# An attention stage on one core: TensorE multiplies the identity by a table before it waits for the prompt's scaled scores, and once at the stage's beginning

## The reference, cut to what matters

```
logits = einsum('bqgrd,bjgd->bgrqj', qn, kn) + bias      # selected and window branch
p = masked_softmax(logits, mask)
o = gates[0] * o_c + gates[1] * o_s + gates[2] * o_w      # o_x = p @ v of each branch
```

## Time and profile before

| | |
|---|---|
| time, median of 3 runs | 1291.38 us (1289.93, 1291.38, 1296.14) |
| span of the profiled execution | 1291.9 us |
| its own time | not among the three; the span lies 0.5 us above their median |
| TensorE busy | 1210.7 us, 94% of the span |
| VectorE busy | 467.1 us, 36% |
| ScalarE busy | 282.3 us, 22% |
| mean granted TensorE clock | 0.982 of full speed |
| attention with this change's places | from about 594 to 788 us of the span |

### The profile page before, as it was taken

The page is one execution under the profiler, slowest core; times in us unless marked ns, Lnnn a source line. Parts: engine busy times, 40 slices in busy tenths (PEclk is TensorE's granted clock), DMA queues, the critical chain, the costliest instruction groups (busy, mean ns, idle before and its releaser), DMA issues.

```text
span 1291.9 us, 38852 instructions
## 1 busy us (share of the span) xinstructions
PE 1210.7 (94%) x16250; PEld 1006.9 (78%) x16250; DVE 467.1 (36%) x1372; ACT 282.3 (22%) x757; POOL 197.9 (15%) x335
## 2 busy tenths in 40 slices
PE   7999999999999998997787879989999999999998
PEld 5887786999999976574345457787898888978876
DVE  2110115677774331004676763421221211212213
ACT  1000003101010021235876861210010000100122
POOL 3012122012340000233345440000000000000000
PEclk9999999999999998999898989999999999999999
DMA  9786879998344264464477776498988879889831
GB/s 311 292 324 238 303 264 314 181 371 311 113 150 175 104 260 177 143 126 137 145 254 217 228 251 252 175 409 330 388 308 346 334 302 394 312 317 367 321 128 37
DMA packets 108352, 326.44 MB, mean 253 GB/s; under 512 B 15512, under 2 KB 33769, under 8 KB 106516
## 3 DMA queue, kind: packets, MB, share of 16 engines
q1 hardware_dynamic: 90868, 263.71, 55.2%
q0 software_dynamic: 16160, 59.96, 15.4%
q10 hardware_dynamic: 1152, 0.30, 0.1%
HBM read 316.65 MB, written 14.52 MB: 256 GB/s over the span
## 4 chain that ended last, share of the span: by engine, by line
PE 87%; DVE 5%; issue 3%; ACT 2%; DMA 1%; POOLq 0%; POOL 0%; ACTq 0%; DVEq 0%
PE bank L1944 20%; PE bank L2543 15%; PE bank L2046 12%; PE pbank L2554 6%; PE bank L2082 6%; PE bank L2000 5%; PE pbank L2543 3%; PE bank L2554 3%; PE bank L2525 3%; PE bank L2150 2%; PE bank L2512 1%; PE bank L2177 1%; PE bank L2317 1%; PE bank L2272 1%; PE pbank L2512 1%
## 5 line engine op out<-in xcount | busy, mean ns | idle before, releaser
L2543 PE MATMUL bank<-X,gring 128*64 128x96 f32 x4608 | 196.0, 247 | 6.1 <-issue 6.1
L2543 PEld LDWEIGHTS bank<-X,gring 128*64 128x64 f32 x4608 | 191.9, 137 | 10.6 <-issue 10.6
L1944 PE MATMUL bank<-aT,gring 128*128 128x288 f32 x768 | 192.7, 410 | 3.5 <-DVE aT L1286 3.5
L1944 PEld LDWEIGHTS bank<-aT,gring 128*128 128x128 f32 x768 | 146.6, 192 | 46.0 <-issue 5.8
L2554 PE MATMUL pbank<-Q,X 128*32 128x256 f32 x1152 | 76.0, 379 | 0.0
L2046 PE MATMUL bank<-aT,gring 128*128 128x144 f32 x528 | 72.1, 286 | 0.0
L1865 DVE TENSOR_TENSOR hT<-hT,bank 128x288 f32<-128x288 f32 x48 | 18.9, 448 | 146.4 <-PE bank L2512 146.4
L2000 PE MATMUL bank<-Q,X 128*64 128x64 f32 x2048 | 63.3, 223 | 7.9 <-issue 7.9
L2000 PEld LDWEIGHTS bank<-Q,X 128*64 128x64 f32 x2048 | 61.3, 138 | 11.9 <-issue 11.5
L1872 DVE TENSOR_TENSOR X<-X,bank 128x96 f32<-128x96 f32 x72 | 18.4, 256 | 141.5 <-ACT X L1232 140.9
L2046 PEld LDWEIGHTS bank<-aT,gring 128*128 128x128 f32 x528 | 67.7, 190 | 0.0
(11 more groups left out here) (380 smaller groups left out, 1814.7 us busy)
## 6 DMA issues: line engine op xcount, KB each, us to landing
gring<-in_moe SPq DMA_DIRECT2D x176, 512.0 KB, 5.7
Q<-in_moe SPq DMA_DIRECT2D x72, 512.0 KB, 7.0
gring<-in_dense_gu SPq DMA_DIRECT2D x44, 512.0 KB, 13.4
Q<-in_cache_cmp POOLq DMA_DIRECT2D x64, 256.0 KB, 5.7
Q<-in_cache_cmp SPq DMA_DIRECT2D x64, 256.0 KB, 5.6
gring<-in_conv_in SPq DMA_DIRECT2D x24, 512.0 KB, 10.2
gring<-in_dense_down SPq DMA_DIRECT2D x16, 704.0 KB, 5.4
gring<-in_ple_gate SPq DMA_DIRECT2D x16, 512.0 KB, 5.6
```

What stands on the lines that cost most here:

```text
L1944: ins = pe.matmul(bank(label, k)[:, 0:T], tile[:, 128 * i:128 * i + 128], rhs[:, i, :], start=i == 0, stop=i == C - 1)
L2543: ins = pe.matmul(m_bank(i, M_GU + f)[64 * w:64 * w + 64, CAP * u:CAP * u + CAP], gslot(("m", 0), 2 * f + u)[:, o:o + 64], ae[:, c, :], st ...
```

## The change: what it does

A helper `kept_busy(dst, n)` issues n multiplications of the 128 x 128 identity by the first 512 columns of `tabP_` into a whole bank. Nothing reads their result; the work that follows starts its own sums in the bank. Eight stand ahead of the three waits at the stage's beginning, behind a wait for the bank of `("sc", 0)` and for `bias_in`. Four stand in each `prompt_transposes(k, 0)`, eight times in all, between `pair_free` and the wait for `pscaled`, into `pbanks[0]`. That is 8 + 8 x 4 = 40 multiplications. Nothing is removed and no other engine's list changes.

```
+            def kept_busy(dst, n):
+                for _ in range(n):
+                    pe.matmul(dst[:, 0:512], ident[:, :], tabP_[:, 0:512], start=True, stop=True)
+
+            bank_free(pe, ("sc", 0))
+            pe.wait_ge(bias_in, 16)
+            kept_busy(bank(("sc", 0)), 8)
             pe.wait_ge(kn_ready, 8)
             pe.wait_ge(q_ready, 8)
             pe.wait_ge(kcn_ready, 3)
...
                 pair_free(pe, k, T0 + i)
+                if i == 0:
+                    kept_busy(pbanks[0], 4)
                 pe.wait_ge(pscaled, 5 * k + (3 if i == 0 else 5))
```

## The result

The changed kernel takes 1313.36 us (median of 4 runs, 1312.55 to 1315.78) against 1292.84 us before in the same comparison: a ratio of 1.0162 with a 95% interval of [1.0137, 1.0188], 17.7 to 24.3 us slower. The prediction said 1300.9 us, 1295.5 to 1305.5. The direction was right; the forecast change, +9.5 us, is less than half of the measured 20.9.

The account below looks back on a forecast made before the run. TensorE, holding 87% of the chain, was taken as the bound. The terms +0.2 - 3.8 + 0.3 + 3.4 + 2.6 + 3.4 + 3.4 sum to +9.5 us: a median of 1300.9 us, range 1295.5 to 1305.5.

Parts of the forecast that it names:

- Price at full clock: TensorE: one added multiplication is two rows of 0.427 us, 0.85 us; four cost 3.41 us.
- Rival D: All places: multiplications are four times as cheap; -0.4 us in all, 1291.0 us; chance 0.05.
- Pair 7: T0 of pair 7: TensorE has no wait there, so the four cost +3.4 us.
- Pairs 1, 3 and 5: T0 there: the four start behind the drain, with nothing left to wait for; +3.4, +2.6 and +3.4 us.
- The cover at pair 3: After pair 3: ScalarE's 1.32 us wait for a DMA hides 0.8 us of the cost, leaving +2.6.
- Pair 6: T0 of pair 6: -0.5 us at full clock, +1.3 if the clock has fallen; taken as +0.3.
- Pair 0: T0 of pair 0: the four prevent the clock's fall over 7.60 us of half-speed work; -3.8 us.
- Rival A: Pair 0: the clock falls all the same; +13.3 us in all, 1304.7 us; chance 0.16.
- Pairs 2 and 4: T0 there: the late start and the half-speed stretch are both covered by VectorE's queue; 0 us.
- Beginning: Stage's beginning: the eight end 1.9 us past the present start, but the clock doesn't fall; +0.2 us.
- Rival B: Half-speed stretches of pairs 1, 3 and 5 go too, saving 4.9 us; +4.6 in all, 1296.0 us; chance 0.15.
- Rival C: Multiplications lie inside the waits everywhere in the loop, odd pairs cost 0.4 each; net -8.6 us, 1282.8 us; chance 0.05.

Follow-up runs that it names:

- e8: Kernel before plus eight multiplications, instead of four, in T0 of pairs 1, 3 and 5 only: 1.0189, +24.4 us.
- e10: Kernel before plus only the four multiplications of pair 7: 1.0031, +4.0 us.
- e3: Kernel before plus only the four multiplications in T0 of pairs 1, 3 and 5: 1.0106, +13.7 us.
- e9: Kernel before plus, at pairs 1, 3 and 5, three multiplications ahead of pair_free and four behind it: 1.0074, +9.6 us.
- e4: Kernel before plus only the four multiplications in T0 of pairs 6 and 7: 1.0045, +5.8 us.
- e16: Kernel before plus only the four multiplications of pair 6: 1.0018, +2.3 us.
- e11: Kernel before plus only the four multiplications of pair 0, first timing: 0.9969, -4.0 us.
- e15: Kernel before plus only the four multiplications of pair 0, second timing: 0.9984, -2.1 us.
- e2: Kernel before plus only the four multiplications in T0 of pairs 0, 2 and 4, first timing: 1.0004.
- e14: Kernel before plus only the four multiplications in T0 of pairs 0, 2 and 4, second timing: 0.9997.
- e13: Kernel before plus only the four multiplications of pairs 2 and 4: 0.9990.
- e1: Kernel before plus only the eight multiplications at the stage's beginning: 1.0004, +0.5 us.
- e5: The kernel before, unchanged, timed once more like a change: 1.0000, runs from 1284.09 to 1296.98 us.
- e6: Kernel before plus three multiplications ahead of pair_free at pairs 1, 3 and 5, into the samples' transposes' bank: 1.0011.

## Why the prediction was wrong, step by step

**Price at full clock: right.** 0.85 us forecast; e8 gives 0.89 from times, pair 7 0.86 from its trace (3.43 us for four). The forecast's row, (7.03 - 0.17) / 16, is 0.429 us and not 0.427, which changes nothing. Rival D falls with it.

**Pair 7: right.** +3.4 forecast; +3.4 in the trace, +4.0 [1.3, 6.7] in e10.

**Pairs 1, 3 and 5: the place was right, the size wrong, and this is the step that failed.** The prediction said "The half-speed stretch lasts until 661.0 in both; only what runs in it changes, so the price is 3.41 at full clock, not more." The stretch did last as long as before. But the step assumed that the transposes, once relieved of the low clock, would give back all that the multiplications lose in it. In the changed kernel the four took 5.2 us at each of the three pairs, 1.8 more than at full clock. From T0 to the next keys it is 3.87 us before (658.20 to 662.07) and 3.38 after (664.21 to 667.59), 0.5 given back; at pairs 3 and 5 it is 4.16 and 4.21 before and 3.38 after, 0.8 given back. What limits it is VectorE: T1 starts 0.1 us behind the last of the four copies in both kernels (661.08 and 666.60), so slow transposes that ran beside the copies had cost little. The prediction named that limit at pair 6 and left it out here. The last copy and T1 of pair 1 in the trace of before:

```profile
660.55 0.42 DVE L1619 COPY X<-pbank 128x256 f32<-128x256 f32 x1
661.08 1.06 PE L2257 MATMUL pbank<-ident,aT 128*128 128x128 f32 x8
```

So the account is 5.2 - 0.5 = +4.7 at pair 1 and 5.2 - 0.8 = +4.4 at pairs 3 and 5, together +13.5; where nearly all four fall into the stretch, as at pair 1 of e3, it is 6.5 - 0.5 = +6.0. e3 measured +13.7 for three where the prediction's terms sum to 9.4; e9, with the four at the high clock, gives +9.6, the price that I had forecast. The two times alone differ by no more than their intervals allow; with the traces of the three places beside them the step is shown.

**The cover at pair 3: nearly absent.** I took 0.8 us from ScalarE's wait for a DMA; at that place +4.5 was lost, with 0.6 back by pair 4.

**Pair 6: too low; the bad case was the usual one.** +0.3 forecast, a value between full clock (-0.5) and a bad case of +1.3 in which the clock has fallen. In e4 and e16 the bad case came as described, with 5.2 us for the four and +1.2 in the trace. In the changed kernel it was worse: the clock fell in TensorE's pause, near 776.1 us, before the four began at 776.92, and stayed low for all of them: 6.5 us, and +2.7 by the table. By time, e16 has +2.3.

**Pair 0: mechanism right, but a gain of one trace, not of the kernel; this is the second step that failed.** -3.8 forecast, -3.4 in the trace. But without the four the long stretch is there in 7 of 11 profiles, so the average gain is 2.3 us by the traces; e11 and e15 measured -4.0 and -2.1, while e2 and e14, with pairs 2 and 4 added, measured +0.5 and -0.4. How much of the gain a time shows stays open. I had reasoned from the one execution as if it were all of them. The Trainium skill (TensorE: Matmul & The Clock Gate, section What's actually happening) says that the slow phase varies from run to run with the same kernel. These profiles agree: the fall at pair 0 lasted some 10.2 us in 7 of 11 and was short or missing in the others. Rival A was no better: the clock didn't fall there in any of the six profiles with the four.

**Pairs 2 and 4: right.** VectorE covers them, e13.

**Beginning: not contradicted** (+0.2 forecast, +0.5 in e1, but with an interval from -2.1 to +3.0 that is no test of it). It is near +2.3 by the two traces with the clock low ahead of it, the changed kernel's and e5's: the wait without the eight is then 3.2 us and not 5.0.

**Rival B** falls twice: the half-speed stretches of pairs 1, 3 and 5 stayed in the changed kernel, and in e6, where they are gone, they are worth nothing measurable, against the 4.9 us which I gave them. **Rival C** falls with the rows at pairs 1, 3 and 5 of the changed kernel: the multiplications start when the drain ends, with no wait behind them.

The change is 20.9 us where 9.5 was forecast. By the four parts e1 to e4 the missing 11.4 are 4.3 in the odd pairs, 4.3 in pairs 0, 2 and 4 (+0.5 for a forecast of -3.8), 2.1 in pairs 6 and 7, 0.3 at the beginning, and 0.4 left over. With the single places put in (0.5 + 13.7 + 2.3 + 4.0 - 2.1, with e15 for pair 0 and pairs 2 and 4 at nothing) the sum is 18.4 us, and 16.5 with e11's -4.0; that is less than 20.9, but within the intervals of the terms. The trace of the changed kernel against that of before has 16.5 of its 19.0 us in the attention's parts: 4.2 more than forecast in the odd pairs, 2.4 more at pair 6, and only 0.4 of gain missing at pair 0, since that one trace of before had the long stretch.

## What to carry to other kernels

Work put in to fill a wait belongs ahead of the last semaphore to be released, not between two of them: find which of the waits ends last at each place, for a helper called eight times may have three of one kind and four of another. Filler that starts behind a pause may itself run at the low clock, here 5.2 to 6.5 us for four that cost 3.4 at full clock, and what it hands on at the high clock is worth only what the next engine in line lets through. A half-speed stretch in one profile is one throw of the dice: before a gain is booked on it, look whether it is there, and as long, in other executions of the same program.

## What the runs showed of the hardware that was not expected

- The kernel before varies by 1% from run to run (1283 to 1299 us over some hundred runs, one far outlier aside). The mean granted clock varies too, from 0.976 to 0.985 in the last 35 of them: the same small multiplications (L2210, L2217) run at 1.00 in one execution and at 0.50 in another (5.4 us of the changed kernel's trace).
- TensorE fully busy didn't always raise the clock. In the kernel before it stayed at 0.50 through 7.60 us of unbroken work on L2272 to L2317; behind the pauses of pairs 1 and 3 it was back within about 3.4 us of the fall.
- The same four multiplications took 3.4, 5.2 or 6.5 us. At pair 6 of the changed kernel nearly all of them lay at 0.50 (the window from 776.2 to 782.9, busy for 5.98 us); those at pair 1 began at 1.00, the clock was 0.50 from 660.1 to 663.4, and they ended at 1.00. How long filler stays slow isn't fixed by the filler.
- Without the four, the fall behind T0 of pair 0 lasted some 10.2 us in seven profiles, 3.4 in three, and was missing in one. The short one cost 0 or 0.5 us, the long one 3.5: most of the short one lay where TensorE waits for VectorE anyway.
